# A Mamba-2 stage reordered: root, reciprocal and first output tiles ahead of splits and taps; decay products ahead of evacuations

## The reference

```python
proj = h @ w_in                       # z, x/B/C, dt
xbc = silu(causal_dwconv(xbc, conv_prev, conv_w, conv_b))    # 4 taps
a_cs = cumsum(dt * a)                 # per chunk of 128 tokens
y = ((C B^T) * decay) @ (x * dt)  +  (C @ h_prev) * exp(a_cs)
y = (y + D * x) * silu(z)
y = y * rsqrt(mean(y * y over one group's 512 channels) + eps) * norm_w
out = y @ w_out                       # added to the residual x
```

## Time and profile before

| | us |
|---|---|
| Median of 3 runs | 2489.83 (2485.96 to 2490.01) |
| Profiled execution | 2488.98 |
| its span | 2487.3 |
| PE busy | 2320.8 (93%) |
| DVE / ACT / POOL busy | 1343.3 / 796.7 / 409.7 |

### The profile page before, as it was taken

One profiled execution on the slowest core, in us unless ns is written; L12 is line 12 of the kernel. 1 busy time (PEld: TensorE's weight loads), 2 busy tenths in 40 slices (PEclk: granted clock), 3 DMA queues, 4 the chain that ended last, 5 costly groups with the idle time before them and its releaser, 6 DMA issues. The chain is left out here.

```text
span 2487.3 us, 44019 instructions
## 1 busy us (share of the span) xinstructions
PE 2320.8 (93%) x18361; PEld 2214.0 (89%) x18361; DVE 1343.3 (54%) x1540; ACT 796.7 (32%) x984; POOL 409.7 (16%) x296
## 2 busy tenths in 40 slices
PE   7999999986779999999999999888989878999997
PEld 7999999873349999999999999887978768999997
DVE  4443445678854443445443345667676766553453
ACT  4222222214332222223222222454545352221223
POOL 0000012680003000003000003010101015545440
PEclk8999999987799999999999999899999989999999
DMA  5323325472532333323323322323232313546442
GB/s 139 84 82 105 85 80 174 149 206 78 151 95 68 85 89 98 90 77 104 97 81 93 102 72 83 99 66 99 69 89 69 94 56 84 139 131 178 132 134 93
DMA packets 430917, 254.86 MB, mean 102 GB/s; under 512 B 12162, under 2 KB 407786, under 8 KB 430752
## 3 DMA queue, kind: packets, MB, share of 16 engines
q1 hardware_dynamic: 430295, 253.08, 36.1%
q10 hardware_dynamic: 508, 0.18, 0.0%
HBM read 239.30 MB, written 14.60 MB: 102 GB/s over the span
## 5 line engine op out<-in xcount | busy, mean ns | idle before, releaser
L220 PE MATMUL PS<-hh,wh 128*128 128x260 f32 x3792 | 775.7, 286 | 27.5 <-DVEq L645 7.9
L220 PE MATMUL PS<-hh,wl 128*128 128x260 f32 x3792 | 769.1, 285 | 0.0
L220 PE MATMUL PS<-hl,wh 128*128 128x260 f32 x3792 | 767.8, 284 | 0.0
L220 PEld LDWEIGHTS PS<-hh,wh 128*128 128x128 f32 x3792 | 591.3, 190 | 39.6 <-issue 22.8
L220 PEld LDWEIGHTS PS<-hh,wl 128*128 128x128 f32 x3792 | 588.7, 190 | 0.3
L220 PEld LDWEIGHTS PS<-hl,wh 128*128 128x128 f32 x3792 | 587.8, 190 | 0.3
L197 DVE TENSOR_TENSOR wl<-raw,wh 128x2048 fp32r<-128x2048 f32 (+2 forms) x194 | 451.7, 2328 | 183.6 <-ACT wh L193 182.3
L193 ACT ACTIVATE wh<-raw 128x2048 fp32r<-128x2048 f32 (+2 forms) x194 | 352.5, 1817 | 313.3 <-PE PS L220 281.7
L220 PE MATMUL PS<-hid_l,wh 128*128 128x260 f32 x1408 | 283.7, 283 | 0.0
L220 PE MATMUL PS<-hid_h,wh 128*128 128x260 f32 x1408 | 283.2, 282 | 0.0
L220 PE MATMUL PS<-hid_h,wl 128*128 128x260 f32 x1408 | 283.0, 282 | 0.0
(11 more groups left out here) (308 smaller groups left out, 2305.3 us busy)
## 6 DMA issues: line engine op xcount, KB each, us to landing
raw<-in_ffn_gate_dram SPq DMA_DIRECT2D x88, 512.0 KB, 4.0
raw<-in_ffn_up_dram SPq DMA_DIRECT2D x88, 512.0 KB, 5.3
raw<-in_ffn_down_dram SPq DMA_DIRECT2D x64, 384.0 KB, 4.0
raw<-in_ffn_down_dram SPq DMA_DIRECT2D x64, 320.0 KB, 3.6
raw<-in_m_in_proj_dram SPq DMA_DIRECT2D x40, 512.0 KB, 5.2
ms_b<-in_state_ssm_dram SPq DMA_DIRECT2D x64, 256.0 KB, 5.0
page<-in_cache_sb_v_dram SPq DMA_DIRECT2D x48, 256.0 KB, 2.9
raw<-in_ab_in_proj_dram SPq DMA_DIRECT2D x20, 512.0 KB, 5.3
```

The lines of the kernel that those rows point to most:

```text
L220: ins = pe.matmul(out, x[:, k0, c:c + m], y[:, k, half * H2:(half + 1) * H2], start=k == 0 and a == 0, stop=k == nk - 1 and a == 2)
```

## The change

Three things, all in `stage_m`:

1. ACT at a group's end: the table set of the root is loaded explicitly, the root comes ahead of the split of the second slot.
2. DVE at a group's end: the reciprocal comes directly behind the evacuation of the last x unit. Two output tiles follow, then the split of the second slot, the third tile, the taps of the last x unit, the fourth tile, the split of the next slot, and four tiles. The scratch of the tiles is `nsc` in groups 0 to 2 (`xraw` still holds the last x unit).
3. DVE in the heads: the products of head hd + 2 come in iteration hd ahead of that iteration's evacuation, in place of iteration hd + 1 behind it.

```diff
-                        hi_static(act, N0 + o_slot(g, 0) + 1)
+                        act.preload_act_table_set("sqrt_and_others")
                         act.wait_ge(S["yms_done"], g + 1)
                         act.activation(halves(sdev[:, :]), PS[:, 6:8, 0:H2], ACT.Sqrt, bias=epst[:, 0:1])\
                             .then_inc(S["ysd_done"], 1)
+                        hi_static(act, N0 + o_slot(g, 0) + 1)
                         if last[0] == "x":
                             both(last)
@@
                         decays(0)
+                        decays(1)
                         between(3)
                         for hd in range(HPG):
-                            if hd + 1 < HPG:
-                                decays(hd + 1)
@@
                             if hd >= 1:
                                 sample_y(hd - 1)
+                            if hd + 2 < HPG:
+                                decays(hd + 2)
                             unit = head_unit(g, hd)
                             if unit and hd < HPG - 1:
                                 evacuate(unit)
@@
                             evacuate(last)
-                            conv(last)
-                        lo_static(dve, N0 + o_slot(g, 0) + 1)
                         dve.wait_ge(S["ysd_done"], g + 1)
                         ch(dve.reciprocal(grs[:, :], sdev[:, :]))
-                        for q in range(2):
+                        def out_tile(q, j):
@@
-                                tmp = xraw[:, j % 2, MT:MT + NT]
+                            tmp = nsc[:, j % 2 * NT:(j % 2 + 1) * NT] if g < MG - 1 else xraw[:, j % 2, MT:MT + NT]
@@
+                        dve.wait_ge(S["ms_prod"], (g + 1) * B)
+                        out_tile(0, 0)
+                        out_tile(0, 1)
+                        lo_static(dve, N0 + o_slot(g, 0) + 1)
+                        out_tile(0, 2)
+                        if last[0] == "x":
+                            conv(last)
+                        out_tile(0, 3)
+                        lo_static(dve, N0 + o_slot(g, 1) + 1)
+                        for j in range(4):
+                            out_tile(1, j)
```

More of the change, by code:

```diff
@@ new lines, in out_tile @@
+                            if j < 3:
+                                dve.wait_ge(S["uo_mm"], 6 * g + 3 * q + j + 1)
+                            else:
+                                dve.wait_ge(w_used, N0 + n + 3)
+                            k = 4 * q + j
+                            b = 2 * (j % 2)
+                            free, cnt = S[f"u{j % 2}_free"], frees(n, j % 2, j // 2) + 1
+                            tmp = nsc[:, j % 2 * NT:(j % 2 + 1) * NT] if g < MG - 1 else xraw[:, j % 2, MT:MT + NT]
@@ new lines, in out_tile @@
+                            dve.tensor_tensor(halves(tmp), PS[:, b:b + 2, 0:H2], halves(grs[:, :]), ALU.mult)\
+                                .then_inc(free, 1)
+                            dve.wait_ge(free, cnt)
+                            ins = dve.tensor_tensor(xT[:, k, :], xT[:, k, :], tmp, ALU.add)
+                            if g < MG - 1:
+                                ch(ins)
+                                return
+                            ins.then_inc(S["x_final"], 1)
+                            if k >= 1:
+                                norm_split_lo(dve, 5, V_NORM[FFN_W[3]], k - 1)
```

## The result

The kernel after takes 2470.18 us, median of 4 runs (2469.33 to 2472.26), beside 2488.08 for the kernel before (2485.96 to 2490.01): ratio 0.9931, 95% interval [0.9915, 0.9947], faster by 17.9 us. A second set of runs gave 2474.47 (2473.20 to 2478.93) beside 2488.84, ratio 0.9950 [0.9937, 0.9964]; where most of those 4 us lie is told at the end of the experiments. Two executions far above all others, one of the kernel before (7835.77 us) and one of an experiment (4513.84), are left out of all medians. The forecast was 2473, 2466 to 2481. The profiled execution after took 2470.99, its span 2468.5.

A forecast was written before the change was run, and what follows sets the result against it. PE, busy 93% of the span, was taken as the bound, so only its waits and the low clock behind them could be won. -18.3 + 0 - 1.0 + 2.3 = -17.0 us gave 2473, range 2466 to 2481.

The forecast's parts named there:

- Part 1: Ends of groups 0 to 2: third tile's wait and low clock go (8.0 us), new 1.9 wait; net 6.1 each, 18.3.
- No clock loss behind the new wait: Seventh tile, groups 0 to 2: the 1.9 us wait adds no clock loss, since waits up to 2.19 left 1.00.
- Part 2: Heads of groups 0 to 2: earlier decay products only move PE's waits; 0, between -1.1 and +1.1 us a group.
- Part 3: Group 3: heads gain 1.0 us; second slot's split, now behind the next norm's first split step, adds 2.29.
- rival c: Group ends: a drain behind the table load brings the root 1.1 us later, 3 x 1.1 more, 2476; chance 0.05.
- (a): Clock falls before the mean as its wait grows to 2.3 us: 1.3 to 3.0 a group, 2477 to 2482; chance 0.14.
- (b): Head waits for decay products really vanish: 6.8 us a group, 20 in three, 2453; chance 0.08.
- (d): Low clock stays from pair 3's wait through last unit, mean and two tiles: 10 us a group lost, 2502; chance 0.03.

The follow-up runs named there:

- the fourth experiment: The whole change, but ACT takes the split of the next slot ahead of the last x unit's SiLU: 2466.71 us.
- the group-end part alone: Kernel before with only ACT's and DVE's new order at the group's end, decay products left as before: 2475.60 us, ratio 0.9947 to the kernel before.
- sixth experiment: The whole change with ACT's split of the second slot back ahead of the root and the table load implicit, DVE's order kept: 2476.57 us.

## Why the prediction was right, point by point

- *Part 1, groups 0 to 2* (6.1 us a group forecast): 6.2, 6.1 and 5.8. The third tile's wait and its low clock went; a wait of 1.71 to 1.72 arose at the seventh tile, where 1.9 was forecast, by the chain taps, SiLU, split, split, product. Moving one link of it (the fourth experiment) took 1.2 us a group of it.
- *No clock loss behind the new wait*: right in the first profile, by luck. The forecast took the wait's length for what decides and read from one wait that up to 2.19 us leave 1.00. The trace it was read from says otherwise: in group 3 a wait of 1.87 was followed by half clock 1.1 us later (PE's row, then the stretch):

```profile
2015.89 0.66 PE L1754 MATMUL PS<-dtxe,dtx 128*64 128x128 f32 x8 [1.87 <-DVE cdec L2187]
...
2017.00:2020.40 3.40, 3.40 (x22) 0.50 0.30 82
```

In the group-end part alone the very wait of 2.19 that it was read from, now 2.21, has 0.53 behind it. Eight profiles hold a wait of 1.71 to 1.75 at the seventh tile, 24 waits in all; three were followed by half clock, two in the group-end part alone and one in the second profile of the whole change, 1.5 to 1.6 us each. The term should have been a price with a chance, not nothing.
- *Part 2* (0, from -1.1 to +1.1 a group): heads +0.3, +0.1 and -0.1. Pair 2's wait went, pair 3's grew to 4.3, and the mean's rose in group 1 to the 2.3 forecast, in group 0 only to 1.66, and in group 2 it fell to 1.21. The waits for products lost 3.7 of 24.1 in total, 2.1 of them in these groups, without shortening the heads. The reason held: splits on ACT set the length. Other kernels moved the heads by about the bound of 1.1 or more: +1.1 to +1.4 when the products of heads 6 and 7 alone were moved, -1.2 to -1.6 when ACT's splits were.
- *Part 3*: the split of 2.29 was all added (group 3's end +1.8, and 2.4 less with the split put back). The heads gave 2.0 in the first profile and 0.3 in the second, where 1.0 was forecast: the last pair's wait was 1.50, with 1.00 behind it, in the first, and 2.59, with 0.50 behind it, in the second. The forecast had counted on the wait's end coming late; the rest is clock. Over all profiles these heads take 62.6 on average with all products moved (nine, 61.76 to 63.79) and 64.2 with none moved (three, 63.78 to 64.62).
- *The drain behind the table load* (rival c, by the Trainium skill, ScalarE: Activation LUTs, section What ACT_TABLE_LOAD costs) did not come: where the root waited for nothing but the load it began 0.01 us behind it (sixth experiment). A root that came 1.9 us later cost 1.5 in the same experiment, so the rival's price was fair. And the load needs no explicit call here.
- *The sum*: -17.0 forecast, -17.9 and -14.4 measured in two sets. Its largest term, the group ends, was right by its mechanism; the falls of the clock are the scatter that it left out, and they make the 3.3 us between the two profiles.
- *Rivals*: (a) did not come at the mean of the whole change (1.00 behind 2.31), and it was the near tie that the forecast called it. In groups 0 to 2 of all 13 profiles the mean ran at 1.00 behind each of 35 waits of up to 2.39 us and fell behind each of the four longer ones (2.66, 3.43, 3.92 and 3.93, in three of the experiments). It then took 5.25 to 5.43 us in place of 3.74, so a fall costs 1.5 to 1.7, near the lower of the rival's prices. (b) did not come: 20.4 us of the head waits are left. (d) did not come.

What stays open: why the same wait at the seventh tile is followed by half clock in one group and not in the next. Its length and its place alone do not decide, as the second profile shows.

## What to carry to other kernels

When a result is late, follow the queue of each engine in front of it for steps that nobody needs yet, and go on past the gain: here the third tile's wait turned into a smaller one at the seventh, found by following DVE and ACT, and most of that could be moved away too. An early release of an engine that only waits for someone else later is worth nothing; find the chain that ends last, here ACT's splits, and shorten that. Give every wait that may drop the clock a price with a chance, and repeat a profile before reading 1.5 us into an edit.

## What the runs showed of the hardware

- Waits of 1.72 and 1.73 us in one execution left PE at 1.00 and at 0.53. In the three falls behind a seventh tile the low clock began 0.6 or 1.4 us after PE had started again and lasted about 3.4 us, 1.5 to 1.6 us lost. At the mean of groups 0 to 2, 35 waits of up to 2.39 us left 1.00, and four of 2.66 to 3.93 us did not.
- The table load that is not asked for runs ahead of the wait of the instruction that needs it (it began at 1822.76, and the root's wait ended at 1824.15), so an explicit load moved nothing (2470.29 beside 2470.18).
